# Gate products of a gated recurrence as four 64x64 tiles, and the filters of long convolutions copied by ScalarE and multiplied by GpSimd

## The chip, the cores and the metric

One core of a Trainium2 chip. The metric is the device time of one execution in microseconds (us), median of several runs. The core's engines are called as the profile calls them: PE (TensorE matmul; PEld is its weight load), DVE (VectorE), ACT (ScalarE), POOL (GpSimd) and SP (SyncE, which here only issues DMAs).

## The reference, cut to what matters

Two transformer-like blocks in fp32 on 1024 rows of width 1024. The change touches two places of the second block: the gates of a linear recurrence (16 heads of width 64, so both gate matrices are block-diagonal), and the filters of two long convolutions.

```python
def rg_lru(xa, w_r, b_r, w_i, b_i, lam, reverse):      # once for each direction
    xh = xa.reshape(B, S, 16, 64)
    r = sigmoid(einsum('bshi,hij->bshj', xh, w_r).reshape(B, S, W) + b_r)
    i = sigmoid(einsum('bshi,hij->bshj', xh, w_i).reshape(B, S, W) + b_i)
    log_a = -8.0 * r * softplus(-lam)
    bx = sqrt(max(1 - exp(2 * log_a), 0)) * (i * xa)
    h = scan of h_t = a_t * h_{t-1} + bx_t             # then gated, w_a_out

def hyena_filters(...):
    h = (h @ w3).reshape(L, 2, 2, 1024)                # order, direction, channel
    return h * decay[:, None, None, :]                 # decay = exp(-t * deltas)

def fftconv(u, k, bias):                               # twice, gated between
    y = irfft(rfft(u, 2 * L) * rfft(k))[:, :L]
    return y + u * bias
```

## The kernel before, in words

The span has these stages: a first block up to 1.25 ms, its combination and norm, the recurrence (`lru_gates_phase`, 1.46 to 2.0 ms), the input projections of the convolutions (2.0 to 2.27 ms), the convolutions (`hyena_phase`, 2.27 to 2.67 ms), a merge, a router and a mixture of experts to the end. All engines run their own instruction streams, ordered against each other by semaphores that the program writes out by hand; nothing is planned at run time.

**The recurrence.** Eight rounds `j`, one for each 128 channels (two heads). In a round PE makes four wide products of 48 matmuls each (`project(j, n)` for AX, AG, GA, GB; fp32 split into three passes of a faster form, L2679), and two gate products, `gates(j, 0)` between GA and GB and `gates(j, 1)` after GB, one for each direction. A gate product (L2893) is four fp32 matmuls, for the two gates `g` and the two halves `t` of the 1024 rows, each with a 128x128 weight tile `w_gate` that holds two heads' 64x64 matrices on its diagonal and zeros beside them (POOL clears both buffers once, L2782). Each fp32 matmul shows as two records. The results fill the four banks of `gate_ps`, which ACT reads by sigmoids (L2961). The operand is `xa`, which DVE makes in `conv(j)` (L3041, L3045) from `a_x`, after its `scan(j - 1)`. ACT's order in a round is `gate_inputs(j)` (L2944, L2949), for the first rounds `round_ya` (L2977), `branch(j, 0)` (L2956, reads GA's product), `lru_gates(j, 0)`, `branch(j, 1)`, `lru_gates(j, 1)`, `decays(j)`.

**The convolutions.** Four passes `n` = 0 to 3 (two convolutions, each in two halves of 512 channels). Transforms are matmuls with tables. The PE order is written out in `program`: U(n, fh) is the spectrum of the input (four slots of 8 fp32 matmuls, halves fh = 0, 1), F(n) makes filters from a small network's hidden layer (`filters`, L4047, 16 matmuls), K(n, fh) is the spectrum of these filters (both halves together 48 matmuls), and I(n) is the transform back (L4094, L4100, 8 banks). F and K occur for n = 1 and n = 3 only; the other spectra were made earlier and are loaded. ACT copies each spectrum slot out of PSUM (L4136) in PE's order. Between U and I stand DVE's `butterflies(n, fh)`: some 24 operations whose inputs lie in SBUF (L3625, L3630, L4152, L4231, L4233), for n = 1, 3 preceded by `filter_butterflies` on K; in `butterflies(n, 0)` the eight results of the pass before (`result`, L4193, out of `inv_ps`) are interleaved. DVE's order is `butterflies(0, 0)`, `filters`, `butterflies(0, 1)`, `butterflies(1, 0)`, `(1, 1)`, `(2, 0)`, `filters`, `(2, 1)`, `(3, 0)`, `(3, 1)`. `filters` (L4172) reads each of the 16 filter tiles of 128x512 from one of two PSUM banks, multiplies it by a decay tile and writes it to `filt`; PE's matmul f waits for DVE's f - 2. Two small operations on one row (L3625, L4178) put in the bias; K waits for them (`end_set`). SP loads four decay tiles ahead and the other four as DVE frees them (L3979, `load_decay` waits `filt_ready`), then, in the order of `program`, the chunks of the next U (L3972). POOL loads and stores the rows of the gated results by DMA.

Of the kernel before, what the change touches and what calls it, by code (L numbers as in the profile page):

```python
# [2683 lines left out]
def lru_gates_phase(nc, block, combined, h_T, w_in, conv_w, conv_b, w_r, b_r, w_i, b_i, lam, w_a_out, ident, sig_T, part_T, gate_T, ahead, next_w):  # L2684
# [7 lines left out]
    NB = range(2)  # L2692
    LAST = N_LRU - 1
# [4 lines left out]
    with Store(nc, "lru") as m:  # L2698

        w = [ahead.w] + [m.parts(f"w{n}", [P, ND, P]) for n, _ in KINDS[1:]]  # L2700
        w_gate = [m.sb(f"w_gate{b}", [P, 2, 2, P]) for b in NB]
        vec_rows = m.sb("vec_rows", [N_ROWS, P])
# [44 lines left out]
        xa_ready = m.sem("xa_ready")  # L2747
        gates_made = m.sem("gates_made")
# [29 lines left out]
        def _(pool):  # L2778
            pool.wait_ge(combined.left, 1)
            pool.memset(a_x[:, :], 0.0).then_inc(cleared, 1)  # L2780
            for b in NB:
                pool.memset(w_gate[b][:, :, :, :], 0.0).then_inc(cleared, 1)  # L2782
# [12 lines left out]
        def _(sp):  # L2795
            def load_vectors():
# [5 lines left out]
                sp.wait_ge(cleared, 3)  # L2802

# [10 lines left out]
            def load_gate(j):  # L2814
                b = j % 2
                if j >= 2:

                    sp.wait_ge(gates_made, 2 * (j - 1))
                for g, src in enumerate((w_r, w_i)):
                    for e in range(2):  # L2820
                        half = slice(e * LRU_D, (e + 1) * LRU_D)
                        sp.dma_start(w_gate[b][half, g, :, half],
                                     src[:, 2 * j + e:2 * j + e + 1, :, :].rearrange("d o p n -> (o p) d n")).then_inc(gate_loaded[b], 16)
# [42 lines left out]
        def _(pe):  # L2866
# [68 lines left out]
        def _(act):  # L2935
            act.wait_ge(cleared, 3)

            def gate_inputs(j):
# [10 lines left out]
                act.activation(a_gate[:, :], flat(out_ps[1][:, :, :]), ACT.Gelu_apprx_tanh).then_inc(gelu_done, 1)  # L2949

# [28 lines left out]
            for j in range(N_LRU):  # L2979
# [5 lines left out]
                if 0 < j <= EARLY:  # L2985
                    round_ya(j - 1)
                branch(j, 0)
# [911 lines left out]
def hyena_phase(nc, block, m, tab, inputs, merge, v_x1, x2_T, z1):  # L3899
# [9 lines left out]
    program = [("U", 0, 0), ("U", 0, 1), ("U", 1, 0), ("F", 1, 0), ("K", 1, 0), ("K", 1, 1), ("I", 0, 0), ("U", 1, 1), ("U", 2, 0),  # L3909
# [29 lines left out]
    filt_made = m.sem("filt_made")  # L3939
    filt_ready = m.sem("filt_ready")  # L3940
    end_set = m.sem("end_set")
# [57 lines left out]
    def _(pool):  # L3999
# [10 lines left out]

        for e in range(2):
            load_gate(e)
        for e in range(BARE * RADIX):
# [4 lines left out]
            if e + 2 < BARE * RADIX:  # L4018
                load_gate(e + 2)

# [13 lines left out]
    def _(pe):  # L4034
        def filters(nth):
# [5 lines left out]
            for t in range(NT):  # L4041
                for d in (SUM, DIFF):
                    f = N_F * nth + 2 * t + d
                    if f >= 2:

                        pe.wait_ge(filt_ready, f - 1)
# [72 lines left out]
    def _(act):  # L4119
        for (what, n, fh), q in place.items():  # L4120
            g = HF * n + fh
# [23 lines left out]
    def _(dve):  # L4145
        c = Chain(dve, step)

        def add(x, y):
            add_to(c, x, y)
# [12 lines left out]

        def filters(nth):
            if nth:

                dve.wait_ge(fwd_made, k_made(MADE[nth - 1], HF - 1))
            for t in range(NT):
                j, r = t // RADIX, t % RADIX
                dve.wait_ge(decay_loaded[t % N_DECAY], 16 * (NT // N_DECAY * nth + t // N_DECAY + 1))
                for d in (SUM, DIFF):  # L4170
                    dve.wait_ge(filt_made, N_F * nth + 2 * t + d + 1)
                    dve.tensor_tensor(filt[:, d, j, r, :], filt_ps[d][:, :], decay_sb[t % N_DECAY][:, :], ALU.mult).then_inc(filt_ready, 1)  # L4172

            dve.wait_ge(filt_ready, N_F * (nth + 1))
            dve.wait_ge(tab.bias_loaded[nth], 16)
            end = filt[0:1, SUM, 0, 0, :]
            add(end, filt[0:1, DIFF, 0, 0, :])
# [385 lines left out]
```

## Time and profile before

| | |
|---|---|
| median of 3 runs | 4062.68 us (4061.16 to 4070.49) |
| the profiled execution | 4070.25 us |
| its span, first to last instruction | 4068.6 us |
| mean granted PE clock | 0.969 |
| busy share of the span: PE, DVE, ACT, POOL | 93%, 71%, 45%, 8% |

The busy shares are means over all stages. What matters here are two stages: the recurrence, where PE is busy 414.69 of the 419 us from 1461 to 1880, and the convolutions, where DVE's operations and PE's take turns in waiting for each other. Times in the rows below are in us from the start of the span, durations in ns where the column says so.

### The profile page before, as it was taken

What the parts mean: (1) busy time and instruction counts of PE and PEld (TensorE: products, weight loads), DVE (VectorE), ACT (ScalarE), POOL (GpSimd) and SP (SyncE); (2) the same over time, 40 slices, a digit from 0 to 9 for tenths busy, and PEclk for the clock granted to TensorE, in tenths of its full rate; (3) what the DMA queues carried; (4) which work ended last, traced back from release to release, by engine and by line L of the source; (5) the groups of instructions that cost most, each with busy time, mean ns of one, the idle gap of its engine ahead of it and who ended that gap; (6) DMA issues with size and microseconds to landing.
All of it is one profiled execution on the core that took longest, in us unless ns stands there. A gap on an engine that the chain in (4) does not pass through costs nothing. (4 is left out here: it accounts for less than half of the span.)

```text
span 4068.6 us, 41958 instructions
## 1 busy us (share of the span) xinstructions
PE 3798.7 (93%) x16652; PEld 2871.6 (71%) x16652; DVE 2868.6 (71%) x2592; ACT 1820.9 (45%) x1686; POOL 309.8 (8%) x286
## 2 busy tenths in 40 slices
PE   8989987899999799999999997889499999999998
PEld 3557765788877677777787443577388888888886
DVE  3645554888887765555244698964698888888887
ACT  3234421777776224433011110210277777777776
POOL 0000000111110100000000000000000101011110
PEclk9999999899999999999999998999799999999999
DMA  3012025899997732223244333143499999999998
GB/s 115 6 54 76 17 90 186 322 398 398 399 399 293 246 112 66 67 68 101 81 133 152 124 114 104 52 148 122 179 364 378 373 381 368 382 369 381 374 378 314
DMA packets 422716, 883.12 MB, mean 217 GB/s; under 512 B 21994, under 2 KB 118609, under 8 KB 421428
## 3 DMA queue, kind: packets, MB, share of 16 engines
q1 hardware_dynamic: 381524, 754.45, 51.3%
q0 software_dynamic: 26896, 97.17, 6.8%
q10 hardware_dynamic: 14160, 29.63, 1.9%
q8 instruction: 94, 1.54, 0.2%
q14 instruction: 42, 0.34, 0.0%
HBM read 784.98 MB, written 96.21 MB: 217 GB/s over the span
## 5 line engine op out<-in xcount | busy, mean ns | idle before, releaser
L2281 DVE TENSOR_TENSOR moe_w_rest<-moe_w_w,moe_upper 128x2048 fp32r<-128x2048 f32 x384 | 862.6, 2288 | 163.1 <-ACT moe_upper L2184 87.0
L2184 ACT ACTIVATE moe_upper<-moe_w_w 128x2048 fp32r<-128x2048 f32 x192 | 357.3, 1909 | 243.5 <-PE moe_y_ps L2148 108.1
L2281 DVE TENSOR_TENSOR moe_w_rest<-moe_w_w,moe_upper_w 128x2048 fp32r<-128x2048 f32 x192 | 431.0, 2286 | 14.6 <-ACT moe_upper_w L2202 14.3
L2202 ACT ACTIVATE moe_upper_w<-moe_w_w 128x2048 fp32r<-128x2048 f32 x192 | 357.5, 1910 | 133.7 <-PE moe_up_ps L2122 77.0
L2192 ACT ACTIVATE moe_upper<-moe_w_w 128x2048 fp32r<-128x2048 f32 x192 | 357.2, 1917 | 0.0
L2122 PE MATMUL moe_up_ps<-moe_upper,moe_x_upper 128*128 128x512 f32 x768 | 311.2, 405 | 0.0
L2122 PE MATMUL moe_gate_ps<-moe_upper,moe_x_upper 128*128 128x512 f32 x768 | 305.8, 398 | 4.7 <-DVE moe_x_rest L2294 4.7
L2148 PE MATMUL moe_y_ps<-moe_upper_w,moe_hidT_upper 128*128 128x512 f32 x760 | 302.2, 398 | 3.6 <-DVE moe_hidT_rest L2299 3.0
L2122 PE MATMUL moe_gate_ps<-moe_w_rest,moe_x_upper 128*128 128x512 f32 x768 | 305.4, 398 | 0.0
L2122 PE MATMUL moe_gate_ps<-moe_upper,moe_x_rest 128*128 128x512 f32 x768 | 304.9, 397 | 0.0
L2122 PE MATMUL moe_up_ps<-moe_upper,moe_x_rest 128*128 128x512 f32 x768 | 304.0, 396 | 0.0
L2122 PE MATMUL moe_up_ps<-moe_w_rest,moe_x_upper 128*128 128x512 f32 x768 | 303.1, 395 | 0.0
L2148 PE MATMUL moe_y_ps<-moe_upper_w,moe_hidT_rest 128*128 128x512 f32 x760 | 300.6, 395 | 0.0
L2148 PE MATMUL moe_y_ps<-moe_w_rest,moe_hidT_upper 128*128 128x512 f32 x760 | 300.6, 395 | 0.0
L2122 PEld LDWEIGHTS moe_gate_ps<-moe_upper,moe_x_upper 128*128 128x128 f32 x768 | 145.4, 189 | 40.7 <-DVE moe_x_rest L2294 5.5
L2148 PEld LDWEIGHTS moe_y_ps<-moe_upper_w,moe_hidT_upper 128*128 128x128 f32 x760 | 142.8, 188 | 43.6 <-DVE moe_hidT_rest L2299 9.6
L3256 ACT ACTIVATE hyin_raw<-hyin_proj 128x1024 f32<-128x1024 f32 x24 | 24.7, 1028 | 328.3 <-PE hyin_proj L2679 328.3
L2122 PEld LDWEIGHTS moe_gate_ps<-moe_w_rest,moe_x_upper 128*128 128x128 f32 x768 | 145.3, 189 | 35.2
L2122 PEld LDWEIGHTS moe_gate_ps<-moe_upper,moe_x_rest 128*128 128x128 f32 x768 | 145.3, 189 | 35.2
L2122 PEld LDWEIGHTS moe_up_ps<-moe_upper,moe_x_rest 128*128 128x128 f32 x768 | 144.2, 188 | 34.5
L2148 PEld LDWEIGHTS moe_y_ps<-moe_upper_w,moe_hidT_rest 128*128 128x128 f32 x760 | 142.8, 188 | 34.5
L2148 PEld LDWEIGHTS moe_y_ps<-moe_w_rest,moe_hidT_upper 128*128 128x128 f32 x760 | 142.8, 188 | 33.8
(592 smaller groups left out, 7663.6 us busy)
## 6 DMA issues: line engine op xcount, KB each, us to landing
moe_w_w<-in_expert_w_dram SPq DMA_DIRECT2D x96, 2048.0 KB, 16.6
moe_w_w<-in_w_gate_dram SPq DMA_DIRECT2D x64, 2048.0 KB, 10.5
moe_w_w<-in_w_up_dram SPq DMA_DIRECT2D x64, 2048.0 KB, 9.9
moe_w_w<-in_w_down_dram SPq DMA_DIRECT2D x64, 2048.0 KB, 9.5
tmp_y_rows<-moe_y ACTq DMA_DIRECT2D x32, 512.0 KB, 6.9
block_w_first<-in_w_in_dram SPq DMA_DIRECT2D x20, 512.0 KB, 3.7
tmp_h<-out_xn POOLq DMA_DIRECT2D x16, 512.0 KB, 3.2
tmp_spectra<-held_K ACTq DMA_DIRECT2D x8, 1024.0 KB, 5.0
```

What stands on the lines that cost most here:

```text
L2122: last = nc.tensor.matmul(out[:, :], lhs[:, k, :], rhs[:, k, :], start=(k == 0 and n == 0), stop=(k == ND - 1 and n == 2))
L2148: last = nc.tensor.matmul(m.y_ps[:, h, :], lhs[:, k, :], rhs[:, k, bass.ts(h, BANK)], start=(start and k == 0 and n == 0), stop=(stop and ...
L2184: act.activation(half(upper1(c), h), half(weights.w1[c % 2], h), ACT.Copy).then_inc(m.w1_rounded, 1)
L2192: act.activation(half(upper3(c), h), half(weights.w3[c % 2], h), ACT.Copy).then_inc(m.w3_rounded, 1)
L2202: act.activation(half(upper2(i, c), h), half(weights.w2[c % 2], h), ACT.Copy).then_inc(m.w2_rounded, 1)
L2281: dve.tensor_tensor(half(rest, h), half(whole, h), half(upper, h).bitcast(F32), ALU.subtract).then_inc(done, 1)
L3256: act.activation(raw[b][:, PAD_L:PAD_L + T], proj_ps[b][:, :, :].rearrange("p a n -> p (a n)"), ACT.Copy).then_inc(raw_ready, 1)
```

## The change

In the recurrence:
- `w_gate` loses its zeros: its last dimension is 64, and the heads of the second gate are stored in the other order (`head = 2 * j + (1 - e if g else e)`). POOL's two clearing memsets and the waits for them go.
- A gate product is eight matmuls of 64x64 weights instead of four of 128x128. For each half of the rows the four (row half, column half) quadrants of PE's array are addressed in turn, and each writes another bank.
- The second gate reads `xa_swapped`, a copy of `xa` with its two 64-partition halves exchanged. ACT makes it in `swap_heads(j)`, two copies of 64x1024, after `round_ya` and before `branch(j, 0)`; PE's gate products wait for it. `vec_rows` moves into the same memory.

In the convolutions:
- ACT copies the filter tiles out of PSUM (`copy_filters`, counted by `filt_copied`), and PE's filter matmuls wait for that copy.
- POOL multiplies them in SBUF by the decays (`decay_filters`) and does the row with the bias in three operations; `filt_ready` and `end_set` come from POOL now. For pass 1 this stands before POOL's loop of stores and loads, for pass 3 behind it.
- DVE's `filters` is gone: its stream runs from one `butterflies` to the next.
- F(1) stands before U(1, 0) instead of behind it, on PE, ACT and SP.

```diff
-        w_gate = [m.sb(f"w_gate{b}", [P, 2, 2, P]) for b in NB]
+        w_gate = [m.sb(f"w_gate{b}", [P, 2, 2, LRU_D]) for b in NB]
+        xa_swapped = m.sb("xa_swapped", [P, T])
...
             def gates(j, d):
                 pe.wait_ge(xa_ready, j + 1)
+                pe.wait_ge(swap_ready, 2 * (j + 1))
...
-                for g in range(2):
-                    for t in range(2):
-                        last = nc.tensor.matmul(gate_ps[:, g, t, :], w_gate[j % 2][:, g, d, :], xa[:, bass.ts(t, BANK)], start=True, stop=True)
+                for t in range(2):
+                    for e, g in ((0, 0), (1, 0), (0, 1), (1, 1)):
+                        rows, cols, half = HALF[e], HALF[1 - e if g else e], t ^ e
+                        last = nc.tensor.matmul(gate_ps[cols, g, half, :], w_gate[j % 2][rows, g, d, :],
+                                                (xa_swapped if g else xa)[rows, bass.ts(half, BANK)], start=True, stop=True)
...
+            def swap_heads(j):
+                act.wait_ge(xa_ready, j + 1)
+                if j:
+                    act.wait_ge(gates_made, 2 * j)
+                for e in range(2):
+                    act.activation(xa_swapped[HALF[1 - e], :], xa[HALF[e], :], ACT.Copy).then_inc(swap_ready, 1)
...
-    program = [("U", 0, 0), ("U", 0, 1), ("U", 1, 0), ("F", 1, 0), ("K", 1, 0), ...
+    program = [("U", 0, 0), ("U", 0, 1), ("F", 1, 0), ("U", 1, 0), ("K", 1, 0), ...
...
+        def decay_filters(nth):                                   # on POOL
+            for t in range(NT):
+                pool.wait_ge(decay_loaded[t % N_DECAY], 16 * (NT // N_DECAY * nth + t // N_DECAY + 1))
+                for d in (SUM, DIFF):
+                    pool.wait_ge(filt_copied, N_F * nth + 2 * t + d + 1)
+                    part = filt[:, d, t // RADIX, t % RADIX, :]
+                    pool.tensor_tensor(part, part, decay_sb[t % N_DECAY][:, :], ALU.mult).then_inc(filt_ready, 1)
...                                                               # then the row with the bias: add, halve, add
+        def copy_filters(nth):                                    # on ACT
+            if nth:
+                act.wait_ge(fwd_made, k_made(MADE[nth - 1], HF - 1))
+            for t in range(NT):
+                for d in (SUM, DIFF):
+                    act.wait_ge(filt_made, N_F * nth + 2 * t + d + 1)
+                    act.activation(filt[:, d, t // RADIX, t % RADIX, :], filt_ps[d][:, :], ACT.Copy).then_inc(filt_copied, 1)
...
-        def filters(nth):                                         # on DVE
-                    dve.tensor_tensor(filt[:, d, j, r, :], filt_ps[d][:, :], decay_sb[t % N_DECAY][:, :], ALU.mult).then_inc(filt_ready, 1)
```

## Rows read from the trace of the kernel before

**Rows 1.** The page, part 1: busy time of each engine.
```profile
PE 3798.7 (93%) x16652; PEld 2871.6 (71%) x16652; DVE 2868.6 (71%) x2592; ACT 1820.9 (45%) x1686; POOL 309.8 (8%) x286
```

**Rows 2.** Windows: length, busy (instructions) of PE, PEld, DVE, ACT, POOL, clock, DMA, GB/s.
```profile
1650.00:1700.00 50.00, 50.00 (x208) 38.70 (x207) 28.90 (x26) 20.72 (x19) 1.06 (x2) 1.00 0.21 66
2296.50:2316.50 20.00, 13.27 (x31) 5.51 (x29) 19.48 (x16) 4.10 (x4) 0.00 (x0) 0.95 0.13 41
2527.60:2553.45 25.85, 25.85 (x61) 11.40 (x60) 25.26 (x18) 6.32 (x7) 0.00 (x0) 1.00 0.28 82
```

**Rows 3.** Timeline of PE, start and length in us: one gate product.
```profile
1661.83 3.59 PE L2893 MATMUL lru_gate_ps<-lru_xa,lru_w_gate 128*128 128x512 f32 x8
1664.86 0.79 PE L2679 MATMUL lru_out<-block_h_T_upper,lru_wgb_upper 128*128 128x512 f32 x1
1665.49 0.40 PE L2679 MATMUL lru_out<-block_h_T_rest,lru_wgb_upper 128*128 128x512 f32 x1
```

**Rows 4.** Timeline of PE in the attention: matmuls on one half of its rows.
```profile
322.81 0.40 PE L1102 MATMUL att_o<-att_in_n_upper,att_wv_rest 128*128 128x512 f32 x1
323.13 0.50 PE L1125 MATMUL att_score<-att_k_upper,att_q_upper 64*128 64x512 f32 x2
...
324.38 0.40 PE L1125 MATMUL att_score<-att_k_upper,att_q_rest 64*128 64x512 f32 x2
...
325.05 0.39 PE L1102 MATMUL att_o<-mixer_in_n_T_rest,att_wv_upper 128*128 128x512 f32 x1
```

**Rows 5.** The same: fp32 matmuls on one half of its columns.
```profile
365.70 0.88 PE L1169 MATMUL att_o<-att_probT,att_v 128*64 128x128 f32 x12
```

**Rows 6.** Timeline of ACT and DVE in the sixth round of the recurrence.
```profile
1653.47 1.28 ACT L2956 ACT_TABLE_LOAD   x1
1662.02 1.02 ACT L2956 ACTIVATE lru_sig_a<-lru_out 128x1024 f32<-128x1024 f32 x1 [7.27 <-PE lru_out L2679]
...
1650.87 3.93 DVE L3045 SCALAR_TENSOR_TENSOR lru_xa<-lru_a_x,lru_vec,lru_xa 128x1024 f32<-128x1024 f32 x3
```

**Rows 7.** One tile's instructions: ns min/median/max of a 64x1024 ACT operation.
```profile
L3607 ACT ACTIVATE filter_hid<-filter_arg x1: 1062/1062/1062, 312.1 to 312.1; 64x1024 f32<-64x1024 f32 x1
```

**Rows 8.** Timeline of PE: the first gate product.
```profile
1510.44 3.70 PE L2893 MATMUL lru_gate_ps<-lru_xa,lru_w_gate 128*128 128x512 f32 x8 [1.67 <-DVE lru_xa L3045]
```

**Rows 9.** Timeline of PE in the convolutions: F(1), K(1), I(0), then F(3), U(3, 0), K(3).
```profile
2307.89 1.88 PE L4047 MATMUL hyena_filt_ps<-hytab_w,hytab_hid_T 128*128 128x512 f32 x4
2317.29 15.68 PE L4047 MATMUL hyena_filt_ps<-hytab_w,hytab_hid_T 128*128 128x512 f32 x28 [7.52 <-DVE hyena_filt L4172]
2335.22 10.05 PE L4058 MATMUL hyena_fwd_ps<-hyena_filt,hytab_tr 128*128 128x512 f32 x19 [2.26 <-issue]
...
2378.16 27.63 PE L4094 MATMUL hyena_inv_ps<-hyena_U,hytab_inv 128*128 128x512 f32 x64
...
2507.09 1.88 PE L4047 MATMUL hyena_filt_ps<-hytab_w,hytab_hid_T 128*128 128x512 f32 x4
...
2523.05 13.90 PE L4058 MATMUL hyena_fwd_ps<-hytab_u,hytab_tr 128*128 128x512 f32 x32
2536.78 41.36 PE L4058 MATMUL hyena_fwd_ps<-hyena_filt,hytab_tr 128*128 128x512 f32 x96
```

**Rows 10.** Timeline of DVE: first filters, first result of pass 0, first of `butterflies(3, 0)`.
```profile
2316.55 1.28 DVE L4172 TENSOR_TENSOR hyena_filt<-hyena_filt_ps,hyena_decay 128x512 f32<-128x512 f32 x2
...
2381.89 0.69 DVE L4193 TENSOR_TENSOR hyena_z<-hyena_inv_ps,hyena_z 128x512 f32<-128x512 f32 x1 [2.25 <-PE hyena_inv_ps L4094]
...
2560.06 1.22 DVE L3625 TENSOR_TENSOR hytab_K<-hytab_K 128x1024 f32<-128x1024 f32 x1
```

**Rows 11.** Timelines of POOL and DVE in the first mixture of experts.
```profile
1022.30 2.17 POOL L2042 COPY moe_idx<-idx_all 128x1 int32 x1 [13.26 <-PE moe_xT_ps L1766]
...
1022.14 4.49 DVE L2281 TENSOR_TENSOR moe_w_rest<-moe_w_w,moe_upper 128x2048 fp32r<-128x2048 f32 x2 [1.66 <-ACT moe_upper L2184]
...
1040.39 0.18 POOL L2042 COPY moe_idx<-idx_all 128x1 int32 x1 [12.93 <-PE moe_xT_ps L1766]
```

**Rows 12.** Groups of POOL by form: busy us, mean ns of one.
```profile
L2782 POOL MEMSET lru_w_gate<- 128x512 f32 x2 | 1.0, 524 | 0.0
```

**Rows 13.** One line's instructions: how long U's chunks take from issue to landing.
```profile
DMA to landing us min/median/max: 3.5/4.2/7.5
```

More of the change, by code:

```diff
@@ L2692, in lru_gates_phase @@
     NB = range(2)
+    HALF = [slice(e * LRU_D, (e + 1) * LRU_D) for e in range(2)]
     LAST = N_LRU - 1
@@ L2820, in load_gate @@
                     for e in range(2):
-                        half = slice(e * LRU_D, (e + 1) * LRU_D)
-                        sp.dma_start(w_gate[b][half, g, :, half],
-                                     src[:, 2 * j + e:2 * j + e + 1, :, :].rearrange("d o p n -> (o p) d n")).then_inc(gate_loaded[b], 16)
+                        head = 2 * j + (1 - e if g else e)
+                        sp.dma_start(w_gate[b][HALF[e], g, :, :],
+                                     src[:, head:head + 1, :, :].rearrange("d o p n -> (o p) d n")).then_inc(gate_loaded[b], 16)
             def load_out(j):
@@ L2986, in _ @@
                     round_ya(j - 1)
+                swap_heads(j)
                 branch(j, 0)
@@ L3939, in hyena_phase @@
     filt_made = m.sem("filt_made")
+    filt_copied = m.sem("filt_copied")
     filt_ready = m.sem("filt_ready")
+    end_added = m.sem("end_added")
+    end_halved = m.sem("end_halved")
     end_set = m.sem("end_set")
@@ L4009, in load_gate @@
             pool.dma_start(z[e % 2][:, :].rearrange("p (j c) -> p j c", j=HJ), residues(v_x1, RESIDUE[i], h, 1)).then_inc(gate_loaded[e % 2], 16)
+        def decay_filters(nth):
[5 more added lines that the diff above has]
+                    pool.tensor_tensor(part, part, decay_sb[t % N_DECAY][:, :], ALU.mult).then_inc(filt_ready, 1)
+            pool.wait_ge(filt_ready, N_F * (nth + 1))
+            pool.wait_ge(tab.bias_loaded[nth], 16)
+            end = filt[0:1, SUM, 0, 0, :]
+            pool.tensor_tensor(end, end, filt[0:1, DIFF, 0, 0, :], ALU.add).then_inc(end_added, 1)
+            pool.wait_ge(end_added, nth + 1)
+            pool.tensor_scalar(end, end, 0.5, None, ALU.mult).then_inc(end_halved, 1)
+            pool.wait_ge(end_halved, nth + 1)
+            pool.tensor_tensor(end, end, tab.bias[nth][:, :], ALU.add).then_inc(end_set, 1)
         for e in range(2):
             load_gate(e)
+        decay_filters(0)
         for e in range(BARE * RADIX):
@@ L4019, in _ @@
                 load_gate(e + 2)
+        decay_filters(1)
         pool.wait_ge(fwd_made, N_ALL_FWD)
@@ L4119, in _ @@
     def _(act):
-        for (what, n, fh), q in place.items():
-            g = HF * n + fh
+        def copy_filters(nth):
[5 more added lines that the diff above has]
+                    act.activation(filt[:, d, t // RADIX, t % RADIX, :], filt_ps[d][:, :], ACT.Copy).then_inc(filt_copied, 1)
+        for what, n, fh in program:
+            if what == "F":
+                copy_filters(MADE.index(n))
+            if what in "FI":
+                continue
+            q, g = place[what, n, fh], HF * n + fh
             if what == "K":
@@ L4161, in sum_w3 @@
             dve.scalar_tensor_tensor(w[:, DIFF, :], w[:, DIFF, :], -2.0, w[:, SUM, :], ALU.mult, ALU.add).then_inc(w3_summed, 1)
-        def filters(nth):
[L4164 to L4171, printed above, removed]
-                    dve.tensor_tensor(filt[:, d, j, r, :], filt_ps[d][:, :], decay_sb[t % N_DECAY][:, :], ALU.mult).then_inc(filt_ready, 1)
[L4174 to L4177, printed above, removed]
-            dve.scalar_tensor_tensor(end, end, 0.5, tab.bias[nth][:, :], ALU.mult, ALU.add).then_inc(end_set, 1)
         def result(n, bank):
@@ L4260, in _ @@
         for n in range(1, NP):
-            if n in MADE:
-                filters(MADE.index(n))
             butterflies(n - 1, 1, None)
```

12 lines of the change are left out of this document (5 added, 7 removed).

## The prediction

> **What bounds the kernel now.** I read the busy shares first [rows 1]: PE is busy 93% of the span, but that is a mean over stages with different limits, so each half of the change is read in its own stage. In the recurrence the first window [rows 2] shows PE busy 50.00 of 50 us at clock 1.00, DVE 28.90 and ACT 20.72. PE alone sets the time there: what PE sheds is won, and what ACT and DVE take on is free as long as they deliver in time. In the convolutions the timelines show two streams that wait for each other. DVE does its butterflies almost without a gap: in 20.00 us before the first filters it is busy 19.48 with 16 operations, and in 25.85 us of `butterflies(2, 1)` 25.26 with 18 [rows 2]. PE in turn waits for the filters, then makes K and I(0) [rows 9], and DVE waits for PE at the first result of pass 0, 2.25 us [rows 10]. So there the question is not how much work DVE loses, but which of the two chains comes last afterwards: DVE's own, or filters, K, I.
>
> **Gate products: what is removed.** A gate product starts at 1661.83. The first wide matmul after it is queued at 1664.86 and the second starts at 1665.49, one step of 0.23 us (the pitch of these matmuls) after the first really began. The block therefore costs 1665.49 - 1661.83 - 0.23 = 3.43 us, eight records of 0.43 each [rows 3]. There are 16 of them.
>
> **What is added on PE.** Eight matmuls of 64x64 are 16 records of the same 512 columns, so 0.43 us each as a stream. All hangs on how many run at once. The trace has both halves of the answer. Two matmuls on the two row halves go together: each x2 row of [rows 4] takes one pitch of 0.23. Two fp32 matmuls on the two column halves, each with its own moving operand, do too: 12 records of 128 columns take 0.88 us, (0.88 - 0.27)/11 = 0.055 us apart, where 128/512 of a gate record's 0.43 would be 0.107 [rows 3, 5]. Four quadrants at once need no operand path that these two cases do not use, so I take four at once: 16/4 x 0.43 = 1.71 us. Going into the tiled form and back costs something: from 322.81 to 325.05 there are one wide matmul, six pairs and one wide matmul, eight pitches of 0.228 = 1.82, measured 2.24, so 0.42 us [rows 4]. A gate product is then 2.13 us and saves 1.30; 16 of them save 20.8 us.
>
> **The copies on ACT.** Nearest row: a 64x1024 ACT operation takes 1.06 us [rows 7], two are 2.1. They stand where ACT waits for GA's product: DVE ends `xa` at 1650.87 + 3.93 = 1654.8, ACT's sigmoid comes at 1662.02 after 7.27 us of idling [rows 6]. The copies end at 1656.9, the gate product needs them at 1661.83: 4.9 us of cover. From the end of one round's last gate product to the next one's first there are only wide products on PE, which do not get faster, so the cover stays. It fails once, in round 0: PE already waits 1.67 us for `xa` [rows 8] and will wait 2.1 more. Nothing else is queued behind that wait that is late. The dropped memsets, 0.52 us each [rows 12], and their waits lie before the first product and I count them at nothing. Sum for the recurrence: -20.8 + 2.1 = -18.7 us. The stages behind it shift as a whole.
>
> **Filters: what DVE sheds.** `filters` occupies DVE from 2316.55 to 2335.05, 18.5 us, and again 18.5 before 2525.3 (16 multiplications that alternate with PE, and two on one row).
>
> **Filters: what POOL costs.** No row shows a POOL operation with two inputs. From below: writing 128x512 takes 0.52 us [rows 12]. From above I take three streams through one port, 1.57 us; between them two input streams, 1.05, which I use, since the operation reads two tiles. By the Trainium skill, "GPSIMD Engine Reference" § 3.1, an add of 2048 elements took 4497 ns, which scales to an estimate of 1.12 us for 512 and would put the whole sum 2.6 us higher. 16 multiplications and the three one-row operations (1.05, 0.52, 1.05) are 19.4 us of POOL work for each set of filters.
>
> **The price that decides: POOL beside DVE.** POOL's copy of 128x1 takes 0.18 us when DVE is idle. Issued 0.16 us after a two-input DVE operation began, it took 2.17 us and ended at 1024.47; that DVE operation, the first of two in 4.49 us, ended at about 1024.43. It waited for the whole operation and got in before the next [rows 11]; the same shows wherever such a copy meets L2281. So a POOL operation that reads SBUF and a DVE operation with two SBUF inputs exclude each other, one operation at a time. I take it as mutual, with strict turns. The Trainium skill, "SBUF — State Buffer" § Who interferes with whom, says so: the second read interface belongs to one of them for a whole instruction. Every operation of the butterflies is of this kind and DVE is busy throughout, so each POOL operation waits for one DVE operation and delays the next.
>
> *First set.* PE comes to F(1) 13.7 us earlier than before, at 2294.2 (U(1, 0) lasts 13.7, as U(3, 0) from 2523.05 to 2536.78 [rows 9]); POOL gets its first turn at 2296.5. 19 turns of POOL are 19.4 us and 0.8 of handing over; the 18 DVE operations between are the 16 up to 2316.5, 20.0 us, and two of 2.3, together 24.7. The end row is ready at 2341.4, and K(1) starts 6.2 us later than its 2335.22 of before [rows 9]. From there K and I(0) run as before, 42.9 us, also from a PE that idled. SP puts the chunks of U(1, 0) behind the fourth of the later decay loads, which waits for POOL's eighth product: 2296.5 + 8.4 + seven DVE operations of 11.0 + 0.3 = 2316.2, and 4.2 to land [rows 13]; U(1, 0) ends by 2336, before 2341.4, so that wait is covered. DVE, 18.5 shed and 20.2 added, comes to the first result of pass 0 at about 2381.4, before the result itself at 2381.89 + 6.2 [rows 10]. Net +6.2 us.
>
> *Second set*, in times of before. F(3) starts at 2507.09; DVE starts `butterflies(2, 1)` at 2508.5, when ACT has copied U(2, 1), so POOL's first turn is at 2510.8. 19.4 + 0.8 + 25.9 for 18 DVE operations [rows 2] end at 2556.9, where K(3, 0) started at 2536.78. PE has idled by then: the first K took 42.9 us for the 41.2 of the second (2536.78 to 2577.99, [rows 9]), so 1.7 more. K(3, 0) is half of 41.2, and its last copy some 1.1: ready at 2556.9 + 20.6 + 1.7 + 1.1 = 2580.3. DVE began on K(3, 0) at 2560.06 [rows 10]. Net +20.2 us.
>
> **Sum.** -18.7 + 6.2 + 20.2 = +7.7 us. The profiled execution, 4070.25 for a span of 4068.6, would take 4078.0; the median of the runs lies 7.6 below it, so the forecast is 4062.7 + 7.7 = 4070. By the low POOL price, K(1) starts at 2332.0, held by U's chunks (-3.2), and the second set costs 10.5: 4051. By the high one, +15.9 and +29.9: 4090.
>
> **Rivals.**
> *No exclusion on this work (faster).* If a long POOL operation doesn't hold DVE up, or yields, the filters end before 2320. F(1) at its old pace of 16.0 us ends at 2310.2, U(1, 0) at 2323.9, K(1) at 2365.1 without the idle start, and the first result 3.7 later, at 2368.8 instead of 2381.89: -13.1. In the second half K(3, 0) is ready at 2558.5 whatever DVE does, so only 1.5 is won; DVE's 17 us go into waiting for K. Total -18.7 - 14.6 = -33.3: 4029. Against it stand rows 11; for it, that they show only a short POOL operation and no DVE operation made longer.
> *The four tiles go two at a time (slower).* Then a gate product is 8 x 0.43 + 0.42 = 3.85 us, 0.42 more than now: the recurrence gives +6.7 + 2.1 = +8.8 and the sum is +35.2: 4098. The point is whether two row halves and two column halves combine, which no row shows. It decides alone whether the change is clearly slower, once the exclusion holds.
> *POOL is passed over (slower).* If it gets only every second gap between DVE's operations, each set lasts some 25 us longer: +50, 4120.
> *The change doesn't do what it says*: not likely for DVE's part, whose 32 operations leave its stream for certain.
>
> **How the numbers follow.** Forecast case 0.50, no exclusion 0.22, tiles in pairs 0.10, POOL passed over 0.08, others 0.10. The range 4029 to 4098 takes in the first three. 0.3%, 12.2 us, is about what a measurement can tell from no change: below 4050.5 is faster, above 4074.9 slower. The forecast case alone spans 4051 to 4090, more than half of it within. Faster: 0.22 and a little of the others, 0.25. Slower: 0.18, a third of the forecast case, and others, 0.37. Same: 0.38.
>
> **What would show it.** Gate records x16 in about 2.1 us with starts in groups of four; a round of 47.8 us instead of 50.4. POOL's products shown with 2 to 3 us each, ending just behind DVE operations, and butterflies around them longer by some 1 us; K(1) at 2341 and K(3, 0) 20 us behind its old place, both counted after the recurrence's shift. Products of about 1.1 us beside unchanged butterflies mean the fast rival. A swap that ends after GA's product would break the recurrence's sum.

## The result and the profile after

The changed kernel takes 4072.61 us (median of 19 runs, 4069.97 to 4080.07), the kernel before, run beside it, 4067.22 us (19 runs). The medians lie 5.4 us apart; the ratio is 1.0016, 95% interval 1.0010 to 1.0022, which is 6.5 us (4.1 to 8.9). The forecast was 7.7 more. Nearly nothing seems to have happened; the trace of the changed kernel shows that two large things did, one for and one against. Its profiled execution took 4071.81 us for a span of 4070.2.

The page, part 1, of the changed kernel; compare [rows 1]:

```profile
PE 3781.2 (93%) x16780; PEld 2854.4 (70%) x16780; DVE 2879.1 (71%) x2556; ACT 1856.7 (46%) x1734; POOL 394.4 (10%) x322
```

DVE has 36 instructions fewer and is busy 10.5 us *longer*. The work that was moved came back as something else.

**The recurrence.** Timeline of PE after the change, start and length in us, around one gate product; it answers [rows 3]:

```profile
1670.17 0.39 PE L2679 MATMUL lru_out<-block_h_T_upper,lru_wgb_rest 128*128 128x512 f32 x1
1670.49 0.65 PE L2894 MATMUL lru_gate_ps<-lru_xa,lru_w_gate 64*64 64x512 f32 x2
1670.50 0.65 PE L2894 MATMUL lru_gate_ps<-lru_xa_swapped,lru_w_gate 64*64 64x512 f32 x2
1670.97 0.59 PE L2894 MATMUL lru_gate_ps<-lru_xa,lru_w_gate 64*64 64x512 f32 x2
...
1671.84 0.60 PE L2894 MATMUL lru_gate_ps<-lru_xa_swapped,lru_w_gate 64*64 64x512 f32 x2
1672.37 0.50 PE L2679 MATMUL lru_out<-block_h_T_upper,block_w_first_upper 128*128 128x512 f32 x1
1672.70 0.40 PE L2679 MATMUL lru_out<-block_h_T_rest,block_w_first_upper 128*128 128x512 f32 x1
```

Two rows of x2 start 0.01 us apart: four tiles at once, every 0.43 us, four times. From the last wide matmul to the second wide one after the tiles there are 2.53 us (1670.17 to 1672.70), of which two steps of 0.23 are wide work: 2.07 us for a gate product where it was 3.43. Timeline of ACT, the copies of `ax` that mark the rounds, first and last of seven; then the swap of round 4, which is covered, since the sigmoid behind it still waits 3.93 us for PE:

```profile
1541.68 1.01 ACT L2946 ACTIVATE lru_a_x<-lru_out 128x1024 f32<-128x1024 f32 x1
...
1697.95 2.15 ACT L2960 ACTIVATE lru_xa_swapped<-lru_xa 64x1024 f32<-64x1024 f32 x2 [1.37 <-DVE lru_xa L3057]
...
1828.07 1.01 ACT L2946 ACTIVATE lru_a_x<-lru_out 128x1024 f32<-128x1024 f32 x1
```

Six rounds take 286.39 us, 47.73 each; before, the same copies lay 302.54 us apart, 50.42 each. That is 2.69 us for two gate products.

**The convolutions.** Timelines of POOL and of DVE in the first set of filters, and of PE; they answer [rows 9, 10]. The first line of POOL sums up all 16 products, the two behind it show two of them alone:

```profile
2278.87 35.20 POOL L4032 TENSOR_TENSOR hyena_filt<-hyena_filt,hyena_decay 128x512 f32<-128x512 f32 x16 [14.72 <-ACT hyena_filt L4161]
...
2291.39 2.24 POOL L4032 TENSOR_TENSOR hyena_filt<-hyena_filt,hyena_decay 128x512 f32<-128x512 f32 x1
2293.59 2.24 POOL L4032 TENSOR_TENSOR hyena_filt<-hyena_filt,hyena_decay 128x512 f32<-128x512 f32 x1
...
2319.35 2.28 POOL L4041 TENSOR_TENSOR hyena_filt<-hyena_filt,hytab_bias 1x512 f32<-1x512 f32 x1
```

```profile
2264.63 2.29 DVE L3637 TENSOR_TENSOR hyena_U<-hyena_U 128x2048 f32<-128x2048 f32 x1 [7.75 <-ACT hyena_U L4183]
...
2290.33 2.17 DVE L4199 TENSOR_TENSOR hyena_U<-hyena_U,hyena_cross 128x1024 f32<-128x1024 f32 x1
2292.54 2.17 DVE L3637 TENSOR_TENSOR hyena_U<-hyena_U,hyena_cross 128x1024 f32<-128x1024 f32 x1
...
2320.55 2.17 DVE L3637 TENSOR_TENSOR hyena_U<-hyena_U 128x1024 f32<-128x1024 f32 x1
2322.75 1.23 DVE L3642 SCALAR_TENSOR_TENSOR hyena_U<-hyena_U 128x1024 f32<-128x1024 f32 x1
...
2368.35 0.69 DVE L4223 TENSOR_TENSOR hyena_z<-hyena_inv_ps,hyena_z 128x512 f32<-128x512 f32 x1 [6.89 <-PE hyena_inv_ps L4128]
...
2565.74 1.23 DVE L3637 TENSOR_TENSOR hytab_K<-hytab_K 128x1024 f32<-128x1024 f32 x1 [18.52 <-ACT hytab_K L4183]
```

```profile
2277.00 14.63 PE L4081 MATMUL hyena_filt_ps<-hytab_w,hytab_hid_T 128*128 128x512 f32 x32
2302.75 16.55 PE L4092 MATMUL hyena_fwd_ps<-hytab_u,hytab_tr 128*128 128x512 f32 x32 [11.12 <-DMA hytab_u<-tmp_v_x]
2321.73 43.05 PE L4092 MATMUL hyena_fwd_ps<-hyena_filt,hytab_tr 128*128 128x512 f32 x96 [2.43 <-issue]
...
2540.81 44.43 PE L4092 MATMUL hyena_fwd_ps<-hyena_filt,hytab_tr 128*128 128x512 f32 x96 [6.59 <-issue]
```

A DVE operation of 128x1024 lasts 2.17 us as long as POOL works and 1.23 us from 2322.75 on, 1.1 us after POOL's last operation has ended. POOL takes one turn for each operation of DVE, and each turn lengthens that operation by 0.94 us: the product of 2291.39 is recorded until 2293.63, 1.13 us after DVE's operation of 2290.33 has ended at 2292.50, and DVE's next one, issued at 2292.54, takes 2.17. PE and ACT have the filters ready in 14.63 us; POOL ends at 2321.63 and K(1) starts at 2321.73. The second set is the same: POOL from 2495.69 to 2540.70, K(3, 0) at 2540.81, and DVE, which had shed work, waits 18.52 us for it.

A milestone helps below: the time from DVE's first butterfly addition (2264.63 here) to PE's first matmul of the merge, which I call **the stretch** of the convolutions. It leaves out what happened earlier in a run.

```profile
2678.24 0.58 PE L2679 MATMUL merge_b_ps<-merge_z_upper,merge_w_upper 128*128 128x512 f32 x1
```

After: 2678.24 - 2264.63 = 413.6 us. Before: 391.7 (2281.77 to 2673.51). So +21.9 in the convolutions, and -17.1 at their start (2264.63 against 2281.77): +4.7.

Executions of the same instructions differ as well, and that limits what such differences say. From PE's first matmul of the recurrence to that butterfly it is 806.7 us in the trace of before and 804.4 in that of `e2_filters` below, which has the same recurrence. The stretch of the changed convolutions is 413.6 us here, 412.7 in `e2_filters` and 410.2 in `e6_diagonal`; K(1) took 43.05 us here and 41.44 in those two. And from the merge to the end, which no edit touches, it is 1392.0 us after and 1395.1 before. This is why the two profiled executions are only 1.6 us apart (4071.81 and 4070.25) with the merge 4.7 later. A difference of some 3 us between two traces, taken alone, shows nothing.

### The profile page after: what moved, and what is told of

The parts are those of the page before. It is cut to its first block and busy times, and to the rows that moved or that the text cites. A ratio compares the mean times of both kernels' runs of the same rounds, so it can differ in the third digit from the quotient of the medians.

```text
span 4070.2 us, 42285 instructions
## 1 busy us (share of the span) xinstructions
PE 3781.2 (93%) x16780; PEld 2854.4 (70%) x16780; DVE 2879.1 (71%) x2556; ACT 1856.7 (46%) x1734; POOL 394.4 (10%) x322
## 6 DMA issues: line engine op xcount, KB each, us to landing
moe_w_w<-in_w_gate_dram SPq DMA_DIRECT2D x64, 2048.0 KB, 10.5
```

## Experiments

### Each half alone

`e1_gates` is the kernel before with the first part of the diff (all up to `swap_heads(j)`), `e2_filters` the kernel before with the rest.

> The kernel before with the recurrence's half of the change alone. My reading of the two traces: each of the eight rounds is shorter by 2.6 to 2.7 us (16 gate products of 2.1 in place of 3.4 us), round 0 gives 2.3 us back for the two copies and runs partly at a lower granted clock. The first butterfly addition on DVE comes 17.1 us earlier in the trace of after, and nothing later depends on it: this kernel takes 17 us less than before (ratio 0.9958). Rival: part of those 17 us is lost or won again behind the recurrence by the place at which the clock or the DMAs fall, 10 us or less of gain.

> The kernel before with the convolutions' half alone. From the trace of after: first result of pass 0 later by 3.6 us and the second set 19.2 us later, both counted after the recurrence's shift, so 22 to 23 us more than before (ratio 1.0055). If the parts add up, this and the kernel with the gates alone sum to the change as a whole, +5.4 us. Rival: if an effect of one half on the other exists, the sum is off by more than 3 us.

Gates alone: 4050.70 us, ratio 0.9962 (0.9948 to 0.9976), 15 us less by the ratio and 17 by the medians. Filters alone: 4088.14 us, ratio 1.0055 (1.0041 to 1.0068), 22 us more by the ratio and 21 by the medians. The stretch is 391.8 with the gates alone, as before, and 412.7 with the filters alone, within 1 us of the whole change. The halves add up (-15 + 22 = +7 by the ratios and -17 + 21 = +4 by the medians, where the whole has +6.5 and +5.4), and no effect of one on the other stands out from the noise: the change is a gain of 15 to 17 us and a loss of 21 to 22.

### Four tiles at once, or smaller tiles?

`e6_diagonal` is the changed kernel, gates on the two diagonal tiles only, no swapped copy:

```diff
-                for t in range(2):
-                    for e, g in ((0, 0), (1, 0), (0, 1), (1, 1)):
-                        rows, cols, half = HALF[e], HALF[1 - e if g else e], t ^ e
+                for g in range(2):
+                    for t in range(2):
+                        for e in range(2):   # rows HALF[e], columns HALF[e]
...
-                swap_heads(j)
```

> The changed kernel, but with the two heads of each gate on the diagonal only, for both gates (tiles of rows e, columns e), without the swapped copy of xa: at most two 64x64 tiles can run at once, eight pairs. Theory, the quarter tiles run four at once in the change because all four quadrants are used: here a gate product is 8 x 0.43 + 0.42 = 3.85 us against 2.1, and the whole takes about 16 x 1.75 - 2.3 (no copies in round 0) = 25 to 26 us more than after (ratio to before about 1.0075). Rival, the tiles' gain comes from the smaller tiles themselves (64 columns or rows cost less): the gate product stays near 2.1 us and the time is that of after or 2 us below it.

Measured: 4096.51 us, ratio 1.0082 (1.0067 to 1.0098), 27 us over the changed kernel by the ratios and 24 by the medians, where 25 to 26 were expected. Timeline of PE in it; the second line is the first two records of the third, shown alone:

```profile
1679.36 0.39 PE L2679 MATMUL lru_out<-block_h_T_upper,lru_wgb_rest 128*128 128x512 f32 x1
1679.68 0.65 PE L2892 MATMUL lru_gate_ps<-lru_xa,lru_w_gate 64*64 64x512 f32 x2
1679.68 3.65 PE L2892 MATMUL lru_gate_ps<-lru_xa,lru_w_gate 64*64 64x512 f32 x16
1683.26 0.50 PE L2679 MATMUL lru_out<-block_h_T_upper,block_w_first_upper 128*128 128x512 f32 x1
1683.60 0.40 PE L2679 MATMUL lru_out<-block_h_T_rest,block_w_first_upper 128*128 128x512 f32 x1
```

The same 16 records now take 1683.60 - 1679.36 - 0.46 = 3.78 us, forecast 3.85: worse than the eight wide records with half of their weights zero (3.43). They start in pairs, so there are eight steps. Two 64x64 tiles cost the full 0.43 us, as four do; all the gain lies in using the four quadrants together, and the swap, which looks like added work, is what makes that possible. The rival "in pairs" of the prediction would have come out as forecast, had it been the case.

### Does POOL's read exclude DVE, or is POOL merely slow?

In `e3_no_read` and `e7_one_input` only POOL's operation differs; both leave out the multiplication by the decays.

```diff
-                    pool.tensor_tensor(part, part, decay_sb[t % N_DECAY][:, :], ALU.mult)
+                    pool.memset(part, 0.0)                               # e3_no_read
+                    pool.tensor_scalar(part, part, 0.5, None, ALU.mult)  # e7_one_input
```

> The changed kernel with each of POOL's 32 multiplications by the decays replaced by a POOL memset of the same 128x512 tile: the multiplication is left out, and POOL writes but reads nothing. Theory, POOL's reads and DVE's operations with two SBUF inputs exclude each other: here no DVE operation is longer than before (128x1024 back at 1.23 us), a memset takes 0.52 us, a set is done as soon as PE and ACT are (some 15 us), K(1) starts about 16 us and K(3, 0) about another 17 us earlier than in the changed kernel: some 33 us less than after, 28 us less than before (ratio 0.993). Rival, POOL is slow of itself or its writes hold DVE up as well: DVE operations stay at 2.17 us and the time stays at that of after, +5 us.

> The changed kernel with each of POOL's 32 multiplications by the decays replaced by a POOL tensor_scalar of the same 128x512 tile by 0.5: the multiplication by the decays is left out, POOL reads one tile and writes one. Theory, any read by POOL takes turns with DVE's operations with two SBUF inputs: POOL's operations still end just behind DVE's, and 16 of them still take some 35 us in the first set, less what the shorter hold saves; DVE operations are longer than before by one POOL operation of one input, some 0.5 us. K(1) comes 16 x 0.45 = 7 us earlier than in the changed kernel, the total is 10 to 14 us below after. Rival, one input does not exclude: DVE operations unchanged, time like with the memset.

`e3_no_read`: 4036.88 us, ratio 0.9931 (0.9916 to 0.9946), 28 us less than before by the ratio, as expected, and 31 by the medians. Timelines of DVE and POOL in it:

```profile
2287.88 1.23 DVE L3637 TENSOR_TENSOR hyena_U<-hyena_U,hyena_cross 128x1024 f32<-128x1024 f32 x1
2289.14 1.23 DVE L3637 TENSOR_TENSOR hyena_U<-hyena_U 128x1024 f32<-128x1024 f32 x1
...
2294.18 2.17 DVE L3637 TENSOR_TENSOR hyena_U<-hyena_U 128x1024 f32<-128x1024 f32 x1
```

```profile
2287.99 0.53 POOL L4032 MEMSET hyena_filt<- 128x512 f32 x1 [0.49 <-ACT hyena_filt L4161]
2288.79 0.53 POOL L4032 MEMSET hyena_filt<- 128x512 f32 x1 [0.27 <-ACT hyena_filt L4161]
...
2293.02 2.23 POOL L4037 TENSOR_TENSOR hyena_filt<-hyena_filt 1x512 f32<-1x512 f32 x1
```

A memset starts and ends in the middle of a DVE operation, in 0.53 us, and DVE's 1.23 us don't change. At 2293.02 POOL issues its first reading operation, on one row: it ends at 2295.25, and the DVE operation issued at 2294.18 takes 2.17. So it is the read that excludes, and one partition costs as much as 128.

`e7_one_input`: 4055.15 us, ratio 0.9975 (0.9966 to 0.9985). Timeline of DVE in it, beside POOL's operations, each recorded with 1.58 us:

```profile
2290.71 1.51 DVE L3637 TENSOR_TENSOR hyena_U<-hyena_U 128x1024 f32<-128x1024 f32 x1
2292.25 1.51 DVE L3642 SCALAR_TENSOR_TENSOR hyena_U<-hyena_U 128x1024 f32<-128x1024 f32 x1
...
2296.90 0.98 DVE L3637 TENSOR_TENSOR hyena_U<-hyena_U 128x512 f32<-128x512 f32 x1
```

One input also excludes and also takes turns, but holds DVE for 0.29 us only. I had guessed 0.5 and a total of 10 to 14 us below after; it was 17.5 (the stretch is 396.8, 16.8 less). The theory stands, the size was off. POOL's 16 operations of the first set still take 30.41 us for 14.63 us of matmuls, since POOL waits for 16 DVE operations whatever its own cost.

### Turns by instruction?

`e10_eight_turns`: POOL does the same products, two tiles in one operation.

```diff
-                for d in (SUM, DIFF):
-                    part = filt[:, d, t // RADIX, t % RADIX, :]
-                    pool.tensor_tensor(part, part, decay_sb[t % N_DECAY][:, :], ALU.mult)
+                both = filt[:, :, t // RADIX, t % RADIX, :]
+                by = decay_sb[t % N_DECAY][:, :].unsqueeze(1).to_broadcast([P, 2, HC])
+                pool.tensor_tensor(both, both, by, ALU.mult)
```

> The changed kernel with POOL multiplying SUM and DIFF of a tile in one operation: 8 of 128x1024 for a set in place of 16 of 128x512, the same work. Theory, strict turns by instruction: POOL waits for 8 DVE operations instead of 16, each of which is 1.9 us longer instead of 0.95; a set takes 8 x (1.9 + 1.5) = 27 us instead of 35, both K(1) and K(3, 0) start some 8 us earlier, some 15 us less than after, 10 less than before (ratio 0.9975). Rival, POOL gets the port at a fixed share of the time and not by instruction: a set lasts 35 us as before, the time is that of after.

Measured: 4053.36 us, ratio 0.9970 (0.9959 to 0.9981), 19 us less than after, where 15 were expected. Timelines of POOL and DVE:

```profile
2276.84 28.25 POOL L4032 TENSOR_TENSOR hyena_filt<-hyena_filt,hyena_decay 128x1024 f32<-128x1024 f32 x8 [16.39 <-ACT hyena_filt L4161]
```

```profile
2289.77 3.25 DVE L4199 TENSOR_TENSOR hyena_U<-hyena_U,hyena_cross 128x1024 f32<-128x1024 f32 x1
```

3.25 - 1.23 = 2.02 us for a turn of twice the size: what DVE loses to the products is about the same as with 16 turns (16 x 0.94 = 15.0 against 8 x 2.02 = 16.2). But POOL waits for 8 of DVE's operations, and the products end 7 us sooner (28.25 for 35.20), in the second set 14 us sooner (25.27 for 39.06; there six of the 16 products had met operations of 128x2048). So the loss to DVE and the lateness of the filters are two costs, and this removes part of the second. The rival, a fixed share of the time, would have left 35 us for the first set: it is out.

### Which of the two costs was it?

`e9_pool_early` moves F(3) and POOL's second set ahead of I(1):

```diff
-               ("I", 1, 0), ("U", 2, 1), ("F", 3, 0), ("U", 3, 0),
+               ("F", 3, 0), ("I", 1, 0), ("U", 2, 1), ("U", 3, 0),
```

> The changed kernel with F(3) and POOL's second set moved ahead of I(1), into the 29.5 us in which PE waits for DVE. What POOL does and what it takes from DVE's operations stays (some 16 times 0.95 us), only what waits for the last product goes. Theory: of the 19 us that the second set costs, most is PE's wait for POOL's last product (DVE waited 18.52 us for K(3, 0)) and not the hold itself. Here I(1) starts 15 to 17 us later (DVE is slower before it), K(3, 0) starts 15 to 16 us earlier, and DVE begins with K(3, 0) at about 2548 instead of 2565.7: some 17 us less than after, 12 less than before (ratio 0.997). Rival: the hold on DVE is the whole cost, wherever it lies: time as after.

Measured: 4056.55 us, ratio 0.9976 (0.9966 to 0.9987), 16.1 us less than after and 12 less than before by the medians. Timelines of PE and DVE in it:

```profile
2468.70 30.00 PE L4129 MATMUL hyena_inv_ps<-hyena_U,hytab_inv 128*128 128x512 f32 x64 [31.95 <-DVE hyena_U L4282]
```

```profile
2548.95 1.23 DVE L3637 TENSOR_TENSOR hytab_K<-hytab_K 128x1024 f32<-128x1024 f32 x1 [0.30 <-ACT hytab_K L4184]
```

This run's stretch begins at 2266.17. Counted from there, I(1) starts 17.3 us later than after the change (202.5 against 185.2), because DVE now loses its time before it, and DVE begins with K(3, 0) 18.3 us earlier (282.8 against 301.1) and waits 0.30 us where it waited 18.52. POOL's turns are as many as ever. The stretch is 393.4, 1.7 us more than before the change. DVE begins with K(3, 0) 4.5 us later than before (282.8 against 2560.06 - 2281.77 = 278.3), and 3.7 of these come from the first set. So nearly all of the second set's 19 us was the wait for POOL's last product; the hold alone, which stays, costs about what DVE had shed.

### The worth of the moved F(1)

`e4_old_order` is the changed kernel with `("U", 1, 0), ("F", 1, 0)` again.

> The changed kernel with F(1) behind U(1, 0) again in PE's, ACT's and SP's order. Theory, the first set's end is POOL's start plus some 43 us of turns and nothing else: POOL starts some 14 us later, K(1) starts some 14 us later, and since DVE waits for the first result of pass 0 already, the whole takes 12 to 14 us more than after (+17 to +19 us against before, ratio 1.0045). Rival, the move is worth nothing since U(1, 0) waits for its chunks behind the decay loads in the changed kernel (11.12 us): U(1, 0) is no longer late, and the time is that of after within 4 us.

Measured: 4083.88 us, ratio 1.0045 (1.0029 to 1.0060), 11.3 us more than after by the medians; the stretch is 426.4, 12.8 more than after. K(1) starts 11.4 us later, counted from the start of the stretch (2330.97 - 2262.52 against 2321.73 - 2264.63). The one reordering in the change is worth 11 to 13 us, though U(1, 0) then waits 11.12 us for chunks that SP loads behind the decays: that wait ends at 2302.75 and the matmuls at 2319.3, 2.4 us before the filters.

### A kernel that beats both

If a turn of POOL costs DVE 0.94 us, DVE can as well do the product itself: both tiles in SBUF, as one of its operations of 128x1024, 1.22 us, are 0.61 for a tile. `e5_sbuf_dve` keeps the gates and ACT's copies, and has F(3) early for PE and ACT. Against the kernel before, `filt` being filled by ACT:

```diff
-                    dve.tensor_tensor(filt[:, d, j, r, :], filt_ps[d][:, :], decay_sb[t % N_DECAY][:, :], ALU.mult)
+                both, by = filt[:, :, j, r, :], decay_sb[t % N_DECAY][:, :].unsqueeze(1).to_broadcast([P, 2, HC])
+                dve.tensor_tensor(both, both, by, ALU.mult)
...
-               ("I", 1, 0), ("U", 2, 1), ("F", 3, 0), ("U", 3, 0),
+               ("F", 3, 0), ("I", 1, 0), ("U", 2, 1), ("U", 3, 0),
...
-        for what, n, fh in program:   # SP
+        for what, n, fh in loads:     # ("I", 1, 0), ("U", 2, 1), ("U", 3, 0), ("F", 3, 0)
```

> Gate products as in the change; in the convolutions ACT copies the filters as in the change, but DVE multiplies them in SBUF, both parts at once (8 operations of 128x1024 for a set, 1.23 us each by the butterflies), POOL does nothing. PE and ACT do F(3) before I(1), where PE waits 29.5 us for DVE; F(1) stays behind U(1, 0); SP loads U(3, 0) before the later decays. Expected by my reading: -17 us from the gates; a set costs DVE about 11.5 instead of 18.5 us, -7 for each of two sets; K(3, 0) no longer waits for F(3), which adds up to -6: 31 to 38 us less than before (ratio 0.991 to 0.9925). Rival: the decay loads t = 4 to 7, each of which waits for a multiplication and lands 4 us later, stretch a set to 18 us again: then only the gates' 17 and some 6 us are left.

Measured: 4040.42 us, ratio 0.9940 (0.9927 to 0.9954): 24 us less than before by the ratio, 25 by the medians, and 32 less than the changed kernel by the medians. In the traces the merge comes 29.7 us earlier than before (2643.84 against 2673.51). I had expected 31 to 38. The stretch is 379.3, 12.4 less than before, where 14 to 21 would have been needed. Timeline of DVE in the second set:

```profile
2484.17 4.62 DVE L4198 TENSOR_TENSOR hyena_filt<-hyena_filt,hyena_decay 128x1024 f32<-128x1024 f32 x4
2491.57 1.23 DVE L4198 TENSOR_TENSOR hyena_filt<-hyena_filt,hyena_decay 128x1024 f32<-128x1024 f32 x1 [2.77 <-issue]
2493.74 3.50 DVE L4198 TENSOR_TENSOR hyena_filt<-hyena_filt,hyena_decay 128x1024 f32<-128x1024 f32 x3 [0.95 <-DMA hyena_decay<-in_filt_decay_dram]
```

The second set takes 14.5 instead of 11.5 us, for the decays came late; and the 6 us for a K(3, 0) that no longer waits were a misreading: DVE did not wait for it before ([rows 10] have no wait at 2560.06), so PE's earlier K is hidden. Two more orders of SP's loads were tried against the 3 us:

```diff
-             ("U", 2, 1), ("U", 3, 0), ("F", 3, 0)
+             ("U", 2, 1), ("F", 3, 0), ("U", 3, 0)                                   # e8_decays_first
+             ("U", 2, 1), ("U", 3, 0) chunks 0 to 2, ("F", 3, 0), ("U", 3, 0) chunk 3   # e11_last_chunk
```

> The kernel with DVE multiplying in SBUF (e5_sbuf_dve), with SP's later decay loads of the second set ahead of the loads of U(3, 0) again. In that kernel's trace DVE waited 2.77 and 0.95 us for decays in the second set, whose loads stood behind a load of U(3, 0) that waits for PE. Theory: these waits go, DVE finishes the set some 3 us earlier and the whole takes 2 to 3 us less than it (ratio to before about 0.993). Rival: now the chunks of U(3, 0) land late, K(3, 0) starts later and DVE waits for it: no gain or some us of loss.

> The kernel with DVE multiplying in SBUF (e5_sbuf_dve), with the second set's later decay loads on SP between the third and the last chunk of U(3, 0). In e5 they stood behind all four chunks and DVE waited 2.77 and 0.95 us for them; in e8 they stood ahead of all four and U(3, 0) waited 12.83 us, DVE 2.45 us for K(3, 0). Theory, only the last chunk waits for PE and only the first three can go ahead freely: both waits go, DVE reaches K(3, 0) 3 us earlier than in e5 by the trace, 3 us less in all (ratio to before 0.993). Rival, another wait of the same size appears, for the last chunk or for K(3, 0): the ratio stays at 0.994.

`e8_decays_first`: 4040.72 us, ratio 0.9940 (0.9927 to 0.9953). Here the rival holds: U(3, 0) waits 12.83 us for its chunks and DVE 2.45 for K(3, 0), and the stretch is 382.1. `e11_last_chunk`: 4040.99 us, ratio 0.9932 (0.9918 to 0.9946). The decays' waits shrink to 0.62 us and DVE reaches K(3, 0) 2.1 us earlier than in e5 (2531.70 - 2264.96 against 2533.35 - 2264.51), but the stretches are 379.1 and 379.3: the gain is gone by the merge. The traces show where. I(3), the last transform, runs in groups between PE's waits for DVE. Windows of its second group in `e5_sbuf_dve` and in `e11_last_chunk`, columns as in [rows 2]:

```profile
2612.77:2619.95 7.18, 7.17 (x32) 6.00 (x32) 6.88 (x7) 0.00 (x0) 0.00 (x0) 1.00 0.00 0
2611.12:2619.98 8.86, 8.86 (x32) 7.18 (x32) 6.90 (x7) 0.00 (x0) 0.00 (x0) 0.81 0.00 0
```

The group starts 2.1 us earlier in e11, counted from the start of the stretch, but at a granted clock of 0.81 instead of 1.00 it takes 1.68 us longer. Why the clock was lower in that execution no run tells. By their times the three kernels can't be told apart.

## Why the prediction was right

- *Gate product, 2.13 us, 1.30 saved.* 2.07 and 1.36. Four at once was an inference from two cases of pairs [rows 4, 5], and e6 shows that it was the decisive one: with pairs the recurrence would have lost. This term came out 1.0 us better than forecast for the 16 products. The 0.42 us for entering and leaving the tiled form hold too (2.07 - 4 x 0.43 = 0.35).
- *Swap covered, 2.1 us in round 0; sum -18.7.* -17.1. The copies took 2.15 us and were covered in each later round. In round 0 PE idled for 3.95 us instead of 1.67, 2.3 more, and the step that the forecast lacked came behind it. Windows and timeline of PE in the changed kernel:

```profile
1505.00:1512.70 7.70, 3.76 (x17) 2.81 (x16) 7.46 (x11) 2.19 (x3) 0.00 (x0) 0.99 0.24 68
1512.70:1516.50 3.80, 3.79 (x17) 1.16 (x18) 3.73 (x5) 2.40 (x3) 0.60 (x1) 0.56 0.03 13
1516.50:1520.00 3.50, 3.50 (x17) 2.83 (x16) 2.52 (x3) 1.96 (x2) 0.00 (x0) 1.00 0.34 136
```

```profile
1512.71 1.12 PE L2894 MATMUL lru_gate_ps<-lru_xa,lru_w_gate 64*64 64x512 f32 x2 [3.95 <-issue]
1513.59 1.09 PE L2894 MATMUL lru_gate_ps<-lru_xa,lru_w_gate 64*64 64x512 f32 x2
```

  The first three are windows with the columns of [rows 2]. After the longer idling the granted clock of the gate product was 0.56, near the lower of the two levels (1.2 GHz), and its steps are 0.85 to 0.88 us instead of 0.43: 1516.54 - 1512.71 - 0.23 = 3.60 us, 1.6 more than the 2.0 of the later ones counted in the same way. In e6, which has no swap, PE idled 1.69 us there and the tiles ran at full pace (3.65 for 16 records, as in its other rounds). So a wait of 2.3 us cost 3.9. It is no accident of one execution: all ten traces with the swap have this idling (3.93 to 3.98 us) and the fall of the clock at this gate product, and the three without the swap (before, e2, e6) idle 1.67 to 1.69 us and keep the full clock. The trace of the changed kernel has a second fall, at the last gate product of the recurrence, behind an idling of 2.33 us. Windows from the start of that product, in the changed kernel and in `e4_old_order`, which has the same recurrence:

```profile
1852.67:1857.37 4.70, 4.70 (x21) 2.38 (x22) 2.50 (x4) 2.15 (x3) 0.00 (x0) 0.64 0.02 5
1852.79:1857.49 4.70, 4.70 (x28) 2.93 (x29) 3.08 (x4) 2.68 (x3) 0.00 (x0) 1.00 0.02 5
```

  The product and the five wide records behind it take 4.70 us here, to the start of the sixth at 1857.37, and 3.14 there (1852.79 to 1855.93), 1.6 us less. Four of the ten traces have this second fall and six don't. Together: 16 x 1.36 = 21.8 saved, 2.3 + 1.6 + 1.6 = 5.5 given back, 16.3, against 17.1 measured; the last 0.8 lie within what executions of the same instructions differ by.
- *First set, +6.2.* +3.6: first result of pass 0 at 2368.35, which is 13.5 earlier than before with 17.1 from the recurrence. From POOL's first turn (2279.32, when DVE's operation of 2277.03 ends) its part took 42.3 us, to 2321.63, instead of 44.9. Of this the mis-sized term is the price of a POOL operation: I took 1.05, and a turn cost 0.94 (2.17 - 1.23), 19 times 0.1. The Trainium skill, "GPSIMD Engine Reference" § 3.1, gives 4497 ns for an add of 2048 elements; scaled to 512, an estimate of 1.12 us. The first product, issued with 0.45 us of DVE's operation left, took 1.58, so about 1.13 of its own: that agrees for the operation. What DVE loses is less, 0.94, and no run tells why. U(1, 0) was covered, as forecast, by 2.4 us instead of 5.4.
- *Second set, +20.2.* +19.2 (2565.74 + 17.1 - 3.6 - 2560.06): From the first turn (2497.34) POOL's part took 43.4 us, to 2540.70, forecast 46.1, by the same term; K(3), for which I took 42.9 us from the first set, took 44.43 and gave 1.5 of it back. e9 confirms the mechanism, a late last product and not the hold.
- *Mutual exclusion in strict turns.* This was the price that decided, read from a POOL operation of 128x1 [rows 11], and it held in both directions: POOL's products ended behind DVE's operations, and DVE's were longer by a turn; that they alternate, instruction by instruction, e10 shows. The Trainium skill, "SBUF — State Buffer" § Who interferes with whom, says that a DVE instruction with two SBUF inputs contends with a GpSimd instruction that reads SBUF and not with one that only writes; the traces of the changed kernel (2.17 for 1.23 us) and of e3 (1.23 unchanged beside memsets) agree on both halves.
- *The rival without exclusion, 4029.* It was priced at -33.3 against before. e3, which comes nearest to that case, came out at -28 by the ratio, -31 by the medians and -33.1 at the merge by the trace.
- *Sum.* -17.1 + 3.6 + 19.2 = +5.7 at K(3, 0), +4.7 at the merge, +5.4 by the medians (+6.5 by the ratio), forecast +7.7. The errors are 1.6 one way and 3.6 the other, and that they nearly cancel is luck. So is part of the agreement with 4070: it stands on a median of three runs before, 4062.68, where 19 runs gave 4067.22; with that base the same sum gives 4074.9. The profiled execution was forecast at 4078.0 and took 4071.81.

The forecast was right because it was resolved into two opposite terms of 17 and 23 us, each right within 4 us. Its case had been given a chance of one half. Nothing in the sum of busy times would have given that.

## What to carry to other kernels

An engine whose reads exclude those of the busy one isn't spare capacity: ask what a moved operation takes from the engine that it is meant to relieve (0.94 us of DVE for each 128x512 product on POOL here, where DVE needs 0.61 itself), and then, as a cost of its own, when the last of the moved operations ends and who waits for it. If such work must be moved, give it in few large instructions and early, where its consumer is late anyway: the two steps brought 19 and 16 us here without any change in the amount of work. The 64x64 tiles paid here only with all four quadrants running together (2.07 us against 3.43 for the wide form and 3.78 for two quadrants), even at the price of a copy.

## What the runs showed of the hardware that I had not expected

- POOL's hold on a DVE operation with two SBUF inputs goes by the elements of a partition and the number of inputs: none for a memset of 128x512, 0.29 us for one input, 0.94 for two, 2.02 for two inputs of 1024. The number of partitions doesn't matter: two inputs on one row, 1x512, held 0.94 as well. The jump from 0.29 to 0.94 for a second input is more than twice, and no run tells why.
- The granted clock of TensorE stood at 1.00 before an idling of 1.67 us and behind it, but at 0.56 behind one of 3.95 us, in the same place of the kernel. 2.3 us of waiting on a saturated engine cost 1.6 more. The length of the idling alone doesn't decide it: behind the 2.33 us before the last gate product, with the same instructions ahead of it, the clock fell in four of ten traces.
